# Delta-rule heads: the inverse applied once per chunk, dense records dealt out two or three per gap, and the query tiles of attention moved ahead of the division

## The reference, cut to what matters

```python
kb = k * beta[..., None]
Lmat = jnp.where(strict, jnp.einsum('bhnid,bhnjd->bhnij', kb, k) * decay, 0.0)
rhs = jnp.concatenate([v * beta[..., None], kb * jnp.exp(gc)[..., None]], axis=-1)
sol = lax.linalg.triangular_solve(eye + Lmat, rhs, left_side=True, lower=True, unit_diagonal=True)
value, k_cumdecay = sol[..., :DV], sol[..., DV:]
...
def step(state, xs):
    a_c, qd, kd, val, kcd, gl = xs
    v_new = val - jnp.einsum('bhcd,bhde->bhce', kcd, state)
    o = jnp.einsum('bhcd,bhde->bhce', qd, state) + jnp.einsum('bhij,bhje->bhie', a_c, v_new)
    state = state * gl[..., None, None] + jnp.einsum('bhcd,bhce->bhde', kd, v_new)
    return state, o
```

## Time and profile before

| | |
|---|---|
| median of three runs | 1900.12 us |
| the profiled execution's own time | 1897.6 us |
| its span, first to last instruction | 1895.5 us |
| mean granted TensorE clock | 0.996 |
| TensorE matmul busy | 1867.9 us, 99% of the span, 10550 instructions |
| VectorE busy | 1210.9 us, 64% |
| ScalarE busy | 788.7 us, 42% |
| GpSimd busy | 301.3 us, 16% |
| chain that ended last, by engine | TensorE 89%, VectorE 6%, ScalarE 2%, issue 1% |

### The profile page before, as it was taken

The page is one execution under the profiler, slowest core; times in us unless marked ns, Lnnn a source line. Parts: engine busy times, 40 slices in busy tenths (PEclk is TensorE's granted clock), DMA queues, the critical chain, the costliest instruction groups (busy, mean ns, idle before and its releaser), DMA issues.

```text
span 1895.5 us, 29611 instructions
## 1 busy us (share of the span) xinstructions
PE 1867.9 (99%) x10550; PEld 1522.6 (80%) x10550; DVE 1210.9 (64%) x1877; ACT 788.7 (42%) x1481; POOL 301.3 (16%) x222
## 2 busy tenths in 40 slices
PE   9999999999999999999999999999999999999997
PEld 8888878888888767777778888888877888888886
DVE  7997554333333877777846846747778568476474
ACT  5234343233233555555534423424547444243242
POOL 0542232111011200001011100101222211011012
PEclk9999999999999999999999999999999999999999
DMA  5233323232222112111113332322411223322231
GB/s 210 89 100 100 134 72 107 90 106 93 100 89 100 45 57 71 56 60 62 51 57 100 100 111 77 103 97 89 134 67 45 73 84 111 100 93 96 89 107 71
DMA packets 46945, 170.47 MB, mean 90 GB/s; under 512 B 5344, under 2 KB 5504, under 8 KB 46720
## 3 DMA queue, kind: packets, MB, share of 16 engines
q1 hardware_dynamic: 45648, 165.12, 26.1%
q10 hardware_dynamic: 1200, 3.95, 0.6%
HBM read 166.94 MB, written 2.11 MB: 89 GB/s over the span
## 4 chain that ended last, share of the span: by engine, by line
PE 89%; DVE 6%; ACT 2%; issue 1%; POOL 0%; DVEq 0%; POOLq 0%; ACTq 0%
PE ps L276 19%; PE ps L278 18%; PE ps L277 18%; PE ps L264 9%; PE ps L266 9%; PE ps L265 9%; PE ps L732 1%; PE ps L757 1%; PE ps L709 1%; DVE scr L1579 1%; DVE scr L1570 1%; DVE Y L1570 1%; ACT Y L1502 0%; PE ps L802 0%; PE ps L741 0%
## 5 line engine op out<-in xcount | busy, mean ns | idle before, releaser
L223 ACT ACTIVATE w_hi<-w_raw 128x1024 fp32r<-128x1024 f32 x302 | 314.9, 1051 | 261.5 <-PE ps L278 172.0
L228 DVE TENSOR_TENSOR w_lo<-w_raw,w_hi 128x1024 fp32r<-128x1024 f32 x253 | 344.6, 1365 | 122.8 <-ACT w_hi L223 122.1
L276 PE MATMUL ps<-A_hi,w_hi 128*128 128x512 f32 x896 | 365.6, 408 | 1.3 <-DVE Y L1069 1.1
L278 PE MATMUL ps<-A_hi,w_lo 128*128 128x512 f32 x896 | 350.5, 391 | 0.0
L277 PE MATMUL ps<-A_lo,w_hi 128*128 128x512 f32 x896 | 349.6, 390 | 0.0
L276 PE MATMUL ps<-B_hi,w_hi 128*128 128x512 f32 x688 | 271.0, 394 | 1.3 <-DVE B_lo L1106 0.9
L278 PE MATMUL ps<-B_hi,w_lo 128*128 128x512 f32 x688 | 268.0, 389 | 0.0
L277 PE MATMUL ps<-B_lo,w_hi 128*128 128x512 f32 x688 | 267.8, 389 | 0.0
L276 PEld LDWEIGHTS ps<-A_hi,w_hi 128*128 128x128 f32 x896 | 168.3, 188 | 37.8 <-DVE Y L1069 2.5
L278 PEld LDWEIGHTS ps<-A_hi,w_lo 128*128 128x128 f32 x896 | 168.5, 188 | 36.1
L277 PEld LDWEIGHTS ps<-A_lo,w_hi 128*128 128x128 f32 x896 | 168.8, 188 | 29.2
(11 more groups left out here) (295 smaller groups left out, 2587.1 us busy)
## 6 DMA issues: line engine op xcount, KB each, us to landing
w_raw<-d_ws SPq DMA_DIRECT2D x304, 512.0 KB, 3.4
X<-d_xT SPq DMA_DIRECT2D x4, 512.0 KB, 7.1
X<-d_xT ACTq DMA_DIRECT2D x1, 2048.0 KB, 8.4
d_out<-X SPq DMA_DIRECT2D x4, 512.0 KB, 2.6
scr<-gc_rows ACTq DMA_DIRECT2D x7, 256.0 KB, 3.1
cst<-d_cst SPq DMA_DIRECT2D x1, 800.0 KB, 11.8
par<-d_par SPq DMA_DIRECT2D x1, 344.5 KB, 3.0
scr<-d_pw SPq DMA_DIRECT2D x1, 256.0 KB, 13.1
```

What stands on the lines that cost most here:

```text
L223: nc.scalar.activation(w_hi[:, c], raw[:, c], ACT.Copy).then_inc(S(f"w_hi{s}"), 1)
L228: nc.vector.tensor_tensor(w_lo[:, c], raw[:, c], w_hi[:, c].bitcast(F32), ALU.subtract)\
L276: pe.matmul(ps[bank][:], w_hi[:, c], hi, start=k == 0, stop=False)
L278: last = pe.matmul(ps[bank][:], w_lo[:, c], hi, start=False, stop=k == total - 1)
```

## The change

The inverse is now applied once per chunk. K·S (the keys by the state) comes first (L785 of the new code); VectorE scales it by the decay and subtracts the values in one instruction, in place in `VR` (L1048); then one matmul with T (L790) gives the negated new value, which VectorE copies out with factor -1 (L1052). `WT`, its two ScalarE copies, the eight T·K' and WT·S products and the four scalings of `KG` go.

Dense work is counted in single records, all written at one line (L684). A level has 2 records in its first gap and 3 in its second, where it had 3 and 3. The scan gets 3 behind each T·VR product, 3 behind each state product and, in heads 1 to 6, one between Q·S and T·VR. The gram products no longer wait for the squares, and use banks 3 and 2. After the scan come 4, 13 and 7 records, where 6, 12 and 12 stood. The last head spreads its 84 records over the same places, and its last block column is opened in two steps (`open_hi`, `open_lo`). VectorE does `conv(1, c+1)` inside the scan; in attention, `q_tile(t + 2)` stands ahead of `normalise(t + 1, 0)`.

```diff
+            def record(s, k, j):
+                if k == 0 and j == 0:
+                    if more:
+                        unit_wait(pe, r, s)
...
+                last = pe.matmul(ps[s % 2 if more else open_bank(s, 4)][:], (w_hi, w_hi, w_lo)[j][:, c],
+                                 tile(pair[j % 2], k), start=k == 0 and j == 0, stop=k == KT - 1 and j == 2)
+                if k == KT - 1 and j == 2:
                     last.then_inc(S(f"unit_done{s}"), 1)
...
             def fill(l, second):
-                dense(1)
-            pe.wait_ge(S("d_sq"), at("d_sq", 2 * NCH))
+                records(3 if second else 2)
...
-            dense(6, 4)
+            records(18, 9, 12)
             pe.wait_ge(S("zeros"), count("zeros", ZEROS))
+            pe.wait_ge(S("d_sq"), at("d_sq", 2 * NCH))
...
-            for i in range(2):
-                pe.wait_ge(S("d_tt"), at("d_tt", 13 + i))
-                if i == 0:
-                    pe.matmul(chunk(ps[3], 0), tt_of(0), chunk(VR, 0), start=True, stop=True).then_inc(S("d_pv"), 1)
-                for c in (2 * i, 2 * i + 1):
-                    last = pe.matmul(chunk(ps[4 + i], c % 2), chunk(KG, c), tt_of(c), start=True, stop=True)
-                last.then_inc(S("d_pw"), 1)
             for c in range(NCH):
+                if c % 2 == 0:
+                    pe.wait_ge(S("d_tt"), at("d_tt", 13 + c // 2))
                 if c:
-                    pe.wait_ge(S("d_wt"), at("d_wt", c // 2 + 1))
                     pe.wait_ge(S("d_s"), at("d_s", c))
-                    pe.matmul(val, chunk(WT, c), ST[c % 2], start=False, stop=True).then_inc(S("d_pv"), 1)
+                    pe.matmul(ps[5][:, 0:P], KQv[:, c, 0, :], ST[c % 2], start=True, stop=True).then_inc(S("d_ks"), 1)
+                    pe.matmul(chunk(ps[6], c - 1), LAv[:, c - 1, 1, :], VN[(c - 1) % 2], start=c == 1, stop=True)
                     pe.matmul(chunk(ps[6], c), chunk(QD, c), ST[c % 2], start=True, stop=False)
-                if c < NCH - 1:
-                    pe.matmul(ps[3 + 4 * ((c + 1) % 2)][:, 0:P], tt_of(c + 1), chunk(VR, c + 1), start=True, stop=False)
+                    records(1, 0, 0)
+                    pe.wait_ge(S("d_sub"), at("d_sub", c))
+                pe.matmul(ps[3 + 4 * (c % 2)][:, 0:P], tt_of(c), chunk(VR, c), start=True, stop=True)\
+                    .then_inc(S("d_pv"), 1)
+                records(3)
                 pe.wait_ge(S("d_vn"), at("d_vn", c + 1))
                 if c < NCH - 1:
                     pe.matmul(ps[2][:, (c % 2 + 1) * P:(c % 2 + 2) * P], chunk(KD, c), VN[c % 2],
                               start=True, stop=True).then_inc(S("d_ps"), 1)
-                if more:
-                    dense(1)
+                    records(3)
...
+            records(4, 0)
             if more:
-                dense(2, 0)
                 token_major_kq(pe, head_count(h + 1))
-                dense(4, 2)
+            records(13, 6, 10)
...
-            if more:
-                dense(4, 2)
+            records(7, 6, 7)
```

```diff
             for c in range(NCH):
+                val = ps[3 + 4 * (c % 2)][:, 0:P]
+                if c:
+                    dve.wait_ge(S("d_ks"), at("d_ks", c))
+                    v.scalar_tensor_tensor(out=chunk(VR, c), in0=ps[5][:, 0:P], scalar=head_col(EGC, h, c),
+                                           in1=chunk(VR, c), op0=ALU.mult, op1=ALU.subtract).then_inc(S("d_sub"), 1)
                 dve.wait_ge(S("d_pv"), at("d_pv", c + 1))
-                v.tensor_copy(VN[c % 2], ps[3 + 4 * (c % 2)][:, 0:P]).then_inc(S("d_vn"), 1)
+                if c:
+                    v.tensor_scalar(VN[c % 2], val, -1.0, None, ALU.mult).then_inc(S("d_vn"), 1)
+                else:
+                    v.tensor_copy(VN[0], val).then_inc(S("d_vn"), 1)
                 if c < NCH - 1:
+                    conv(1, c + 1)
...
+            pe.wait_ge(S("o_hi"), count("o_hi", HEADS))
             for s in range(SLOTS):
-                part_blocks(pe, open_bank(s, 4), s, pairB, KT - 1, KT, wait=o_wait(pe)).then_inc(S(f"unit_done{s}"), 1)
+                open_hi(pe, rnd(U_AOUT, 0), s, pairB, KT - 1, 4)
+            pe.wait_ge(S("o_lo"), count("o_lo", HEADS))
+            for s in range(SLOTS):
+                open_lo(pe, s, pairB, KT - 1, 4)
...
-                    normalise(t + 1, 0)
                     if t + 2 < KT:
                         q_tile(t + 2)
+                    normalise(t + 1, 0)
```

More of the change, by code:

```diff
@@ L704, in fill, with records @@
+            tiles = KT if more else KT - 1
+            at_record = 0 if h else 3 * KT
+            def records(n, n_first=None, n_last=None):
+                nonlocal at_record
+                n = n_first if not h and n_first is not None else n
+                n = n_last if not more and n_last is not None else n
+                for _ in range(n):
+                    record(at_record // (3 * tiles), at_record // 3 % tiles, at_record % 3)
+                    at_record += 1
             def fill(l, second):
-                dense(1)
```

82 lines of the change are left out of this document (22 added, 60 removed).

## The result

The changed kernel takes 1917.72 us (median of four, 1914.84 to 1922.09), the kernel before 1900.13 us: a ratio of 1.0089 with a 95% interval of 1.0074 to 1.0104. The forecast was 1902.4 us with a range up to 1909.0, so it was wrong. The profiled execution took 1919.29 us and its span was 1917.4, 21.9 us above that of the kernel before.

The account below looks back on a forecast made before the run. TensorE, busy 99% of the span, was taken as the bound. The terms summed to +2.3 us on the profiled 1897.6, so 1899.9, and 1902.4 as median of the runs; range 1893.5 to 1909 for 8 times in 10.

Parts of the forecast that it names:

- C: Heads 1 to 6, before L790: the inverse's write stands behind unit 1's evacuation on VectorE; +1.45 us a head.
- D: Level 1: gram products come earlier against VectorE, so TensorE waits 0.56 us a head, about 1.9 in the last head.
- E: Gaps of two records in levels 2 to 5, a tie with ScalarE's copies: +0.1 us a head.
- F: Level 6's first gap, a record shorter while ScalarE's copies are not: +0.2 us.
- A: The scan's small matmuls: 21 products become 17 per head, -0.90 us.
- End of the last head: From L821 to L264: the next unit's split waits longer for unit 0's last record; +0.5 us, bounds 0 to 1.
- Attention: Query tile made ahead of the first division: L1379's 1.47 us wait goes, nothing new is late; -1.5 us.
- B: The scan's old waits and restarts, taken as covered by records: -0.84 us in each of heads 1 to 6.
- The clock: Rival 3: granted clock falls to half behind the new waits in six heads; about 1910 to 1914 us, chance 0.06.
- Rival 2: Levels' gaps of two records are too short for ScalarE's copy: 1909.6 us at the upper bound, chance 0.14.
- a head over 1.5 us longer: Sign in the profile after: if gram to gram takes over 1.5 us longer, E is wrong.

Follow-up runs that it names:

- e1: The changed kernel with VectorE's evacuation of the next head's unit 1 moved behind the inverse's writes and first VN copy, later convolution steps one chunk back: 1910.83 us.
- e2: The changed kernel with three records in both gaps of every level in heads 0 to 6, taken from those behind the scan: 1908.90 us.
- e3: The changed kernel with 12 records again between the output's transposes and the gram products, and 12 first records for 9 in head 0: 1917.34 us.
- e6: The changed kernel with gate GT and scaled queries QD made on VectorE inside level 1, displaced half splits one place later: 1911.66 us.
- e12: The kernel before with four unread repeats of a gram product in head 0's idle ahead of level 1's first products: 1899.04 us, ratio 0.9995.
- e11: The changed kernel run again unaltered: 1913.64 us, ratio 1.0073.
- e9: The changed kernel with unread gram products filling TensorE's idle ahead of level 1, six in head 0, three in the last head: 1908.43 us, ratio 1.0042.
- e5: The changed kernel with 3 records in the first gap and 2 in the second at levels 1 to 5, 3 and 3 at level 6: 1907.35 us.
- e8: The changed kernel's algebra with the old layout of dense records in heads 0 to 6, last head as changed: 1912.89 us, ratio 1.0065.

## Why the prediction was wrong

**C, the wait in front of L790** stood in its place, in heads 1 to 6, from its cause: forecast 1.15 and 0.1 to restart, measured 1.14 from ready to start (0.97 of idle in the list). e1 and e2 took it away. The 0.2 for the late VN copy was not there: L795 came at its time. The rule that the VectorE queue is first in, first out (the Trainium skill, "TensorE: Matmul & The Clock Gate", "Architectural detail: the array is 16× 32×32, not 1× 128×128") agrees with the trace: VectorE stood in front of the evacuation until 854.88, while the products that the write needs (L776) had begun at 852.98 and lasted 0.96 us.

**D, level 1**: forecast 0.56 at L753, measured 0.44 there and 0.23 more in front of L728, which I had given as on time: 0.7 where 0.56 stood. e3 and e6 took the wait of L753 away.

**E and F**: 0.1 and 0.2 forecast, about 0.2 and 0.25 measured. **A**: -0.90, no measurement by itself; the bill closes with it. **End of the last head**: +0.5 forecast, +0.6 measured. **Attention**: -1.5 forecast, -0.9 measured; that "nothing new is late" failed, as the last tile waits for the division.

**B failed.** I took all three chains of the scan as covered, -0.84 a head. The margins were 0.08 for K·S and 0.02 for the state update. K·S's way to VectorE's start was longer than the row that I had taken for it: 857.84 to 858.37 is 0.53 us, against my 0.42. With 0.35 and 0.05 behind it that makes 0.93, against 0.90 of cover. For the state update I had followed only VectorE's own queue (copy, convolution step, update). The update also needs the state product L795, which stands behind three records, and from there it is again 0.53 (859.80 to 860.33) and 0.40 to the release: 0.93, against 0.91. The kernel before had even 0.64 at such a place (L802 at 806.90, its update at 807.54). Behind each such lateness TensorE loses another 0.1 before it runs evenly; I had priced that restart in C and left it out here. Waits and restarts are 0.96 us a head, so the term is +0.12. That alone is 6 us in six heads. The text allowed for 0.3 a head. The sizes are read from the trace; no run restored the cover alone.

**The clock failed as a rival of 0.06**, and stood at nothing in the sum. I tied it to the six waits in front of L790 and argued from one stretch in the last head that had stayed at full clock; in e12 the same instructions ran into half clock. It fell behind one of the six in each profile of the changed kernel, and mostly behind two other waits, which D had made longer, 2.05 to 2.87 us in head 0 and 0.55 to 1.55 in the last head, and stayed down for up to 13.7 us. For head 0 I took the old cost over with the old wait. Cost: 10.4 to 11.3 us of the 21.9 between the profiled executions; in the medians, 5.2 us between e11 and e9. How much of it an execution pays is chance, and the profiled one had paid much. With the waits of heads 0 and 7 filled the kernel is still 8.0 us slower than before (e9), just inside the upper end of my range; what is left there above the forecast is mostly B.

So the sum was +2.3 and the profiled execution +21.9. The missing 19.6 us are 10.4 of clock, 5.8 of B in six heads, about 0.6 in attention, and the rest head 0 and the small terms. Rival 2, the short gaps, stood for the slower side and was not what happened: e5 gives it a few tenths a head. My sign for it, a head over 1.5 us longer, did appear (1.6), and pointed at the wrong step: E was 0.1 off, B 0.96.

## What to carry to other kernels

In a kernel bound by TensorE, filler records are a budget: a record moved into one gap is missed in another, and a chain covered by less than 0.1 us isn't covered, so count at what record each unit ends and what stands behind its evacuation before moving anything. Follow every input of the waiting instruction, its product as well as its engine's queue, and add a restart behind each lateness. Where TensorE's single waits grow (here to 1.0, 1.5 and 2.9 us), price the clock behind them as well, with a range, since one profile at full clock doesn't show that the next stays there. Unread matmuls in such idle time kept the clock up in head 0 and in the last head (e9), and cost nothing that the runs show.

## What the runs showed of the hardware that I had not expected

The granted clock went to half behind single waits of TensorE of 1.0 to 2.9 us, and how long it stayed there differed between executions of one program: 13.7 and 10.3 us in head 0 for the same instructions, 3.5 us in e1, and in e8, with a wait of 2.2 us there, it didn't fall at all. In e12 it fell behind a row of waits of 0.55 us and less. From the start of a small product to the start of the VectorE instruction that waits for it, the traces have 0.42, 0.53 and 0.64 us at different places. At half clock a record starts every 0.43 us (675.36 to 675.79 in head 0 of the changed kernel) where it is 0.23 at full clock, and a level of small products takes 4.38 us instead of 2.60. The kernel before has this too, once in head 0.
